# Seventeen projection blocks by seven half-size products, none beside the convolution; identity, rows and first weights load ahead of the other constants

## The reference

```python
for l in range(2):                       # first block
    h = rmsnorm(x, g[0])
    y = even_mixer(h, ...) if l % 2 == 0 else odd_mixer(h, ...)
    x = x + rmsnorm(y, g[1])
    x = x + rmsnorm(square(relu(rmsnorm(x, g[2]) @ w1)) @ w2, g[3])
# even: p = h @ w_in (5120 columns), gated linear attention and retention, y @ w_out
# odd:  p = h @ w_in (3080 columns), a convolution over positions, an mLSTM, y @ w_out
# second block
z = modulate(rms_norm(x, g), sh1, sc1) @ w_in      # 5120 columns: q k v, xb bg cg, gates
x = x + ga1 * ((gate_a * (attention(q, k, v) @ w_pa) + gate_b * (conv(xb, bg, cg) @ w_pb)) @ w_o)
x = x + ga2 * moe(modulate(rms_norm(x, g2), sh2, sc2))  # 32 experts, two for each row
```

## Time and profile before

| | |
|---|---|
| time, median of 3 runs | 1543.97 us (1541.52 to 1544.95) |
| time of the profiled execution | 1541.41 us |
| its span, first to last instruction | 1539.6 us |
| PE busy | 1301.7 us, 85% |
| DVE busy | 439.4 us, 29% |
| ACT busy | 194.2 us, 13% |
| POOL busy | 73.9 us, 5% |

### The profile page before, as it was taken

One profiled execution on the slowest core, in us unless ns is written; L12 is line 12 of the kernel. 1 busy time (PEld: TensorE's weight loads), 2 busy tenths in 40 slices (PEclk: granted clock), 3 DMA queues, 4 the chain that ended last, 5 costly groups with the idle time before them and its releaser, 6 DMA issues.

```text
span 1539.6 us, 12320 instructions
## 1 busy us (share of the span) xinstructions
PE 1301.7 (85%) x5308; PEld 706.0 (46%) x5308; DVE 439.4 (29%) x615; ACT 194.2 (13%) x274; POOL 73.9 (5%) x77
## 2 busy tenths in 40 slices
PE   7899998999999997999999999998746646646646
PEld 3455546886444453888444445445312212212212
DVE  3355122456442432246544130214101001001001
ACT  2321111111001321111001113101100000000000
POOL 0126101000000000000001100000000000000000
PEclk9999998999999999999999999999878868878788
DMA  9433332885453314587453443365699999999996
GB/s 333 145 110 123 151 110 101 309 299 192 164 178 105 133 76 158 182 299 264 168 187 136 171 156 110 123 259 231 283 429 427 428 427 427 427 428 427 427 428 258
DMA packets 93462, 376.72 MB, mean 245 GB/s; under 512 B 6976, under 2 KB 7520, under 8 KB 81504
## 3 DMA queue, kind: packets, MB, share of 16 engines
q1 hardware_dynamic: 92696, 373.80, 62.8%
q0 software_dynamic: 576, 2.10, 0.4%
q10 hardware_dynamic: 136, 0.04, 0.0%
HBM read 374.88 MB, written 1.05 MB: 244 GB/s over the span
## 4 chain that ended last, share of the span: by engine, by line
PE 74%; DMA 19%; DVE 2%; SPq 2%; issue 1%; ACT 1%; POOL 0%; POOLq 0%; DVEq 0%; ACTq 0%
PE PS L619 24%; PE PS L786 15%; PE PS L796 12%; DMA weights<-in_w 10%; DMA proj_rows<-in_w 9%; PE PS L644 8%; PE PS L1006 5%; PE PS L1037 2%; PE PS L589 1%; SPq L455 1%; PE PS L700 1%; PE PS L970 1%; PE PS L756 1%; PE PS L978 1%; PE PS L830 0%
## 5 line engine op out<-in xcount | busy, mean ns | idle before, releaser
L619 PE MATMUL PS<-weights,normalised 128*128 128x512 f32 x832 | 365.1, 598 | 2.4 <-DVE normalised L1354 2.2
L619 PEld LDWEIGHTS PS<-weights,normalised 128*128 128x128 f32 x832 | 158.1, 192 | 196.6 <-issue 196.6
L1006 PE MATMUL PS<-weights,arena 128*32 128x512 f32 x512 | 140.1, 708 | 114.2 <-DMA weights<-in_w 81.3
L786 PE MATMUL PS<-normalised,weights 128*128 128x256 f32 x1024 | 224.0, 382 | 1.7 <-DVE normalised L1354 1.7
L786 PEld LDWEIGHTS PS<-normalised,weights 128*128 128x128 f32 x1024 | 196.1, 192 | 29.4 <-DVE normalised L1354 2.3
L796 PE MATMUL PS<-weights,arena 128*128 128x512 f32 x384 | 167.4, 592 | 0.0
L644 PE MATMUL PS<-weights,arena 128*128 128x512 f32 x288 | 125.1, 593 | 5.4 <-issue 4.5
L1006 PEld LDWEIGHTS PS<-weights,arena 128*32 128x32 f32 x512 | 36.3, 128 | 185.5 <-issue 158.1
L796 PEld LDWEIGHTS PS<-weights,arena 128*128 128x128 f32 x384 | 73.0, 190 | 91.0 <-issue 90.9
L1006 PE MATMUL PS<-arena 128*32 128x512 f32 x208 | 72.3, 723 | 22.7 <-DMA proj_rows<-in_w 22.7
L1813 DVE TENSOR_TENSOR arena<-arena,PS 128x512 f32<-128x512 f32 x8 | 8.4, 1047 | 291.3 <-PE PS L1006 291.3
(11 more groups left out here) (282 smaller groups left out, 1088.5 us busy)
## 6 DMA issues: line engine op xcount, KB each, us to landing
weights<-in_w SPq DMA_DIRECT2D x41, 2048.0 KB, 25.7
weights<-in_mlp_w SPq DMA_DIRECT2D x32, 2048.0 KB, 7.9
arena<-in_w SPq DMA_DIRECT2D x21, 2048.0 KB, 24.9
proj_rows<-in_w SPq DMA_DIRECT2D x20, 2048.0 KB, 25.4
proj_rows<-in_w_ada SPq DMA_DIRECT2D x12, 2048.0 KB, 8.2
weights<-in_ev_w_in SPq DMA_DIRECT2D x10, 2048.0 KB, 8.3
weights<-in_w_in SPq DMA_DIRECT2D x10, 2048.0 KB, 7.9
normalised<-in_w SPq DMA_DIRECT2D x10, 2048.0 KB, 24.8
```

What stands on the lines that cost most here:

```text
L619: last = mm(PS[:, 2 * (n % 2) + tt, :], HT[:, k, tt * P:(tt + 1) * P], wn(s)[:, k, :], start=(k == 0), stop=(k == KT - 1))
L786: last = mm(PS[:, 4 + 2 * h + j // 2, (j % 2) * T:(j % 2 + 1) * T], wn(s)[:, k, j * P:(j + 1) * P], HT[:, k, :], start=(k == 0), stop=(k = ...
L1006: last = mm(PS[CAP * x:CAP * (x + 1), 4 + kind, :], XG[:, k, CAP * x:CAP * (x + 1)], w[:, k, :], start=(k == 0), stop=(k == KT - 1), tile_ ...
```

## The change

Seventeen of the 26 blocks (`SEVEN`: even blocks 1, 2, 3, 8, 9; odd blocks 1, 2, 3; blocks 1 to 9 of the second block) are multiplied by `seven_block`. Rows and columns are halved: four halves of the rows (128 rows x 512) and four of the block (512 x 256). DVE makes four sums of row halves once in each layer (`row_halves`) and four sums of weight halves for each block (`col_sums` three, `last_sum` one; one of them in place, the others in the fourth slot). PE makes seven products of four matmuls each, 128 x 128 against 128 x 256, 28 matmuls. Some products stay in PSUM and others are added onto them, so ACT reads four partial sums out while PE goes on (`part`), PE waits for those reads, DVE adds them (`part_sums`), and ACT does the rest (`finish`). The even blocks 4 to 7 and the odd blocks 4 and 5 stay as they were, and so does the first block of each layer.

The order of the even layer changes with it: block 3 now runs before the levels begin, the products of `hg_b` write banks 6 and 7, and the levels move one block on. At the start the identity is loaded alone and ahead of x, the first weights ahead of five of the rows, and the rest of the constants after the mask tables. Two gain rows (`ga_in`) are loaded in the first MLP. Expert block 0 is no longer loaded early; the slots of the first three expert blocks change places.

```diff
+SEVEN = ([B_EV_IN + b for b in (1, 2, 3, 8, 9)] + [B_OD_IN + b for b in range(1, 4)]
+         + B_IN2_AT[1:])
+SUM_BUFS = ((0, 2, 3), (3, 0, 2), (2, 3, 0))
-MOE_SLOTS = (3, 6, 7, 1, 4, 5, 2, 0, 8)
+MOE_SLOTS = (6, 7, 3, 1, 4, 5, 2, 0, 8)
...
+            sp.dma_start(IDN, A["keep"][:, 0:P]).then_inc(sem("const_in"), 16)
             for tt in range(TT):
                 sp.dma_start(X[:, tt, :], xv[:, tt, :]).then_inc(sem(f"x{tt}_in"), 16)
-            sp.dma_start(CK[:, :], A["keep"]).then_inc(sem("const_in"), 16)
-            row_loads(nc.sync, 0)
...
                 if b == 0:
+                    row_loads(nc.sync, ROW_LOADS[7:])
                     ld("lb_in", LB, A["hg_lower_bound"].partition_broadcast(P))
                 elif b == 1:
                     ld("mix_in", MX, A["mix"])
+                    ld("mix_in", CK[:, P:C_KEEP], A["keep"][:, P:C_KEEP])
...
-                if b == 3:
-                    sp.wait_ge(sem("block_used"), B_MLP1 + MLP_B)
-                    expert_load(0)
...
-            for j in range(1, 3):
-                sp.wait_ge(sem("block_used"), B_PB + 1)
-                expert_load(j)
+            sp.wait_ge(sem("block_used"), B_PB + 1)
+            expert_load(0)
+            expert_load(1)
             sp.wait_ge(sem("block_used"), B_IN2_AT[9] + 1)
+            expert_load(2)
             expert_load(3)
...
+            def seven_block(b):
...
+                pe.wait_ge(sem(f"slot{s}_full"), fulls(b))
+                pe.wait_ge(sem("row_sums"), 1 + (b >= B_OD_IN) + (b >= B_IN2))
+                pe.wait_ge(sem("col_sums"), 2 * m + 1)
+                pe.wait_ge(sem("proj_taken"), n - 1)
+                product(x, HT[:, 0:4, 0:P], b11, True).then_inc(sem("proj_part"), 1)
+                product(y, s1, t1, True).then_inc(sem("proj_part"), 1)
+                pe.wait_ge(sem("part_read"), 4 * m + 1)
+                product(x, s2, t2, False).then_inc(sem("proj_part"), 1)
+                pe.wait_ge(sem("part_read"), 4 * m + 2)
+                product(y, s4, b22, False)
+                pe.wait_ge(sem("part_read"), 4 * m + 3)
+                product(x, s3, t3, False).then_inc(sem("proj_part"), 1)
+                product(z, HT[:, 4:8, 0:P], b21, True).then_inc(sem("proj_part"), 1)
+                pe.wait_ge(sem("part_read"), 4 * m + 4)
+                pe.wait_ge(sem("col_sums"), 2 * m + 2)
+                product(x, HT[:, 4:8, P:T], t4, False).then_inc(sem("block_used"), 1)
...
-            for b, levels in ((3, (1,)), (4, (2, 3)), (5, (4, 5)), (6, (6, 7)), (7, (8,)), (8, ())):
+            for b, levels in ((4, (1, 2)), (5, (3, 4)), (6, (5, 6)), (7, (7, 8))):
                 proj_block(B_EV_IN + b)
...
+            def finish(b, cols, func=ACT.Copy, scale=1.0):
...
+                act.wait_ge(sem("part_sum"), m + 1)
+                act.wait_ge(sem("block_used"), b + 1)
+                last = a(PR[:, 1, cols:cols + T], PS[:, 2 * (n % 2), 0:T], func, scale=scale)
+                if func != ACT.Copy or scale != 1.0:
+                    top, low = PR[:, 0, cols:cols + NB], PR[:, 1, cols + T:cols + NB]
+                    a(top, top, func, scale=scale)
+                    last = a(low, low, func, scale=scale)
...
+            def col_sums(b):
...
+                dve.wait_ge(sem(f"slot{s}_full"), fulls(b))
+                if m:
+                    dve.wait_ge(sem("proj_part"), 5 * m - 4)
+                link(v.tensor_tensor(t3, b22, b12, ALU.subtract))
+                if m:
+                    dve.wait_ge(sem("proj_part"), 5 * m - 2)
+                link(v.tensor_tensor(t2, t3, b11, ALU.add))
+                tell(v.tensor_tensor(b12, b12, b11, ALU.subtract), "col_sums", 2 * m + 1)
...
+            def last_sum(b):
...
+                if m:
+                    dve.wait_ge(sem("proj_part"), 5 * m - 1)
+                v.tensor_tensor(t4, wn(slot_of(b))[:, 4:8, 0:T], t2, ALU.subtract).then_inc(sem("col_sums"), 1)
...
+            def part_sums(b, cols):
...
+                dve.wait_ge(sem("part_read"), 4 * m + 4)
+                dve.wait_ge(sem("proj_part"), 5 * m + 5)
```

More of the change, by code:

```diff
@@ L346, in block_program, with row_loads @@
         ]
-        def row_loads(queue, part):
-            for at, col, src in ROW_LOADS[part::2]:
+        def row_loads(queue, loads):
+            for at, col, src in loads:
                 queue.dma_start(AR[at:at + src.shape[0], col:col + P], src).then_inc(sem("rows_in"), 16)
@@ L889, in _ @@
                 logits(h)
[L890 removed]
+            seven_block(B_IN2_AT[5])
             pe.wait_ge(sem("at_s"), 8)
@@ L1095, in _ @@
             evac(0, ACT.Silu)
-            evac(NB, ACT.Sigmoid)
+            parts(B_EV_IN + 1)
+            finish(B_EV_IN + 1, NB, ACT.Sigmoid)
+            part(B_EV_IN + 2, 0)
+            part(B_EV_IN + 2, 1)
             act.wait_ge(sem("hg_qT_raw"), 1)
@@ L1123, in _ @@
             a(S01, PS[:, 4, :].rearrange("p (h t) -> p h t", h=4), ACT.Copy).then_inc(sem("hg_s01"), 1)
-            even_evac(8)
+            parts(B_EV_IN + 8)
+            finish(B_EV_IN + 8, 8 * NB, ACT.Silu)
             def squares(src, dst, wait, v, name):
@@ L1135, in _ @@
                   PS[:, 4 + half, :].rearrange("p (h t) -> p h t", h=4), ACT.Copy).then_inc(sem("ret_T"), 1)
-            even_evac(9)
+            parts(B_EV_IN + 9)
+            finish(B_EV_IN + 9, 9 * NB, ACT.Silu)
             n_mix = [0]
@@ L1200, in _ @@
             evac(0, ACT.Copy)
-            evac(NB, ACT.Copy)
+            parts(B_OD_IN + 1)
+            finish(B_OD_IN + 1, NB)
             act.wait_ge(sem("gates_raw"), 1)
@@ L1210, in _ @@
             a(GR[:, 2, :], GR[:, 1, :], ACT.Ln, bias=1.0).then_inc(sem("g_softplus"), 1)
-            evac(2 * NB, ACT.Copy)
+            parts(B_OD_IN + 2)
             for q in range(4):
@@ L1231, in _ @@
             mlp_square(1)
-            for b in range(2):
-                evac(b * NB, ACT.Copy)
+            IN = B_IN2_AT
+            evac(0, ACT.Copy)
+            parts(IN[1])
+            part(IN[2], 0)
+            part(IN[2], 1)
+            finish(IN[1], NB)
             a(HB.rearrange("p (a b) -> p a b", a=2), PR[:, :, 0:1024], ACT.Square).then_inc(sem("mix_sq"), 1)
-            for b in range(2, 4):
-                evac(b * NB, ACT.Copy)
+            part(IN[2], 2)
+            part(IN[2], 3)
+            parts(IN[3])
+            finish(IN[2], 2 * NB)
             for q in range(4):
@@ L1243, in _, with logit_exps @@
                   PS[:, 4 + q, :].rearrange("p (h t) -> p h t", h=4), ACT.Copy).then_inc(sem("qk_T"), 1)
-            evac(4 * NB, ACT.Copy)
-            act.wait_ge(sem("at_max"), 1)
-            for h in range(AH):
+            finish(IN[3], 3 * NB)
+            parts(IN[4])
+            def logit_exps(h):
                 a(AS[:, h, 0:P], AS[:, h, 0:P], ACT.Exp, bias=ST[:, 32 + h:33 + h], scale=AD ** -0.5,
@@ L1250, in _ @@
                   accum_out=ST[:, 56 + h:57 + h]).then_inc(sem("at_exp"), 1)
-            evac(5 * NB, ACT.Copy)
+            part(IN[5], 0)
+            part(IN[5], 1)
+            finish(IN[4], 4 * NB)
+            act.wait_ge(sem("at_max"), 1)
+            for h in range(2):
+                logit_exps(h)
+            part(IN[5], 2)
+            for h in range(2, 4):
+                logit_exps(h)
+            act.wait_ge(sem("at_max"), 2)
+            logit_exps(4)
+            part(IN[5], 3)
+            for h in range(5, AH):
+                logit_exps(h)
+            finish(IN[5], 5 * NB)
             for q in range(6):
@@ L1255, in _ @@
                     .then_inc(sem("at_pT"), 1)
-            evac(6 * NB, ACT.Sigmoid)
+            parts(IN[6])
             for tt in range(TT):
@@ L1260, in _ @@
                   ACT.Copy).then_inc(sem("u_T"), 1)
-            evac(7 * NB, ACT.Sigmoid)
+            part(IN[7], 0)
+            part(IN[7], 1)
+            finish(IN[6], 6 * NB, ACT.Sigmoid)
+            part(IN[7], 2)
+            part(IN[7], 3)
             for tt in range(TT):
@@ L1269, in _ @@
                     .then_inc(sem("u_T"), 1)
+            finish(IN[7], 7 * NB, ACT.Sigmoid)
             for b in range(8, 10):
-                evac(b * NB, ACT.Sigmoid)
+                parts(IN[b])
+                finish(IN[b], b * NB, ACT.Sigmoid)
             for half in range(2):
@@ L1644, in _ @@
             norm(GM[:, 0, :], MC[:, 0, :])
+            IN = B_IN2_AT
+            row_halves(IN[0])
+            for b in range(1, 3):
+                col_sums(IN[b])
+                last_sum(IN[b])
+            part_sums(IN[1], NB)
             dve.wait_ge(sem("mix_sq"), 4)
```

203 lines of the change are left out of this document (169 added, 34 removed).

## The result

Before 1542.74 us median of 4 runs, changed kernel 1526.58 (1525.64 to 1529.26): ratio 0.990, 95% interval 0.9883 to 0.9917. The change makes the kernel 16 us faster where 28.5 were forecast; 1526.58 lies 0.6 us above the range (1507 to 1526), and the gain is a little more than half of the forecast. The profiled execution took 1525.64 us with a span of 1523.8, against 1539.6: 15.8 us between the two profiles.

What follows compares the result with a forecast made beforehand. PE was taken to set the time until the expert-weight stream starts near 1093 us. 27.4 + 6.8 - 1.4 - 1.8 - 2.0 - 0.75 - 0.55 + 0.8 = 28.5 us saved, forecast 1514 us, range 1507 to 1526.

Steps and rivals of the forecast that it cites:

- The blocks: Seventeen seven-product blocks take 12.12 us each on PE instead of 13.73, saving 1.61 each, 27.4 us in all.
- Even layer, order: With block 3 ahead of the levels, PE's 9.99 us there become 3.6, plus 0.36 at the next block: 6.8 saved.
- The bound of 2 us for block 8's sums: Even block 8: DVE's sums beside POOL's rotations cost PE nothing, 2 us at the slowest.
- The Silu behind them: Finish of even block 8: its table load can no longer be made in advance, costing 0.15 us.
- Start: PE's start at 14.28 us was taken as unchanged, between 1 us sooner and 1 later.
- Odd layer: Its seven-product blocks save 4.8 us, less a 1.4 us wait in block 2: 3.4 us.
- the wait at the gates: Odd block 2: ACT works on the gates before its first read, so PE waits 1.4 us.
- Second block: Nine seven-product blocks, with waits of 1.8, 2.0 and 0.75 us and 0.8 won at block 7: 10.3 us gained.
- 5.87: Second block: the us POOL needs from the sums of squares of q and k to the norm.
- The stages without an edit: Both MLP stages and the stage from output product to experts hold no seven-product block; forecast change 0.
- The rival of half the gain: PE at half clock around waits near 893 and 897, several products waiting for reads: 18 us less gain, 1532; chance 0.12.
- the wait for q and k: Second block, `qk_ready` at 893.1 us, ahead of block 4: PE waits 1.8 us.

Runs made afterwards that it cites:

- e5: Changed kernel with all 26 projection blocks plain, keeping the new order, start and expert slots; 1536.0 us, ratio 0.9971 to the kernel before.
- e3: Changed kernel with the old start: all constants in one load, rows split over both queues ahead of the first weights; 1525.19 us, ratio 0.9886.
- e13: e11 with the five rows that SP loads put back ahead of the first weights; 1514.17 us, ratio 0.9814.
- e11: Changed kernel with even block 8 and block 3 of the second block plain (fifteen seven-product blocks); 1515.33 us, ratio 0.9830.
- e4: Changed kernel with block 3 of the second block plain (16 seven-product blocks); 1520.83 us, ratio 0.9858.
- e6: Changed kernel with matmuls on constants keeping PE busy at stage boundaries and the modulation's one-column products moved earlier; 1531.02 us, ratio 0.9930.
- e7: Kernel before the change with the same edit as e6; 1546.62 us, ratio 1.0033.
- e2: Kernel before the change run once more, nothing edited; one run, 1545.4 us.
- e8: Changed kernel with even block 8 plain; 1521.96 us, ratio 0.9869.
- e9: Changed kernel with two matmuls on constants (1.7 us) behind the odd layer's block 0; 1531.1 us, ratio 0.9926, its profile from an execution at 1524.39.
- e12: e11 with six matmuls on constants ahead of the transposes of both MLPs; 1516.6 us, ratio 0.9829.
- e1: Changed kernel run once more, nothing edited; 1527.4 us, ratio 0.9902 to the kernel before.
- e10: Changed kernel with four matmuls on constants (3.5 us) behind the odd layer's block 0; 1532.04 us, ratio 0.9929.
- e14: Changed kernel with all blocks of the second block plain, the eight seven-product blocks of the other two layers kept; 1535.09 us, ratio 0.9939.

## Why the prediction was wrong

**The blocks** (27.4 counted): right. Each takes 12.09 us, and seven products start one after another without a loss where the reads are on time. What the sum lacked stands around them, in two steps: the clock at the stage boundaries, and POOL's rate.

**Even layer, order** (6.8): right. 3.57 us instead of 9.99; e5 has it apart, 229.02 us from block 0 to the first MLP against 235.01, 6.0, though its blocks 0 and 1 take 30.66 us and not 29.40. (The prediction's upper end, 7.2 "if not even the 3.6 show", is a slip: its own rows give 9.99 + 0.36.) The bound of 2 us for block 8's sums was right and its value, 0, wrong: DVE turned to them 5.5 us ahead of the block and not 8, at 2.2 us each, and PE waits 1.31. The Silu behind them costs 6.33 - 5.92 = 0.4 and not 0.15.

**Start** (0, within 1): 1.24 in the profile. The rows behind 2 MB of weights land too late; x and its norms do not set that time. How much of it reaches the end stays small: the whole old start gives back 0.3 us at the first MLP (e3), the five rows alone 1.4 (e13), part of it by the clock in block 0 (13.97 us against 15.67 in e11).

**Odd layer** (3.4): 3.97, with 1.6 us for the wait at the gates (1.4 forecast). The half-clock stretch that made block 4 last 15.63 us before is gone, 1.7 us not foreseen; block 0 costs 0.7 more by the clock.

**Second block** (10.3): 5.4. Timeline of PE in the changed kernel around `qk_ready`:

```profile
884.76 3.28 PE L618 MATMUL PS<-constants,proj_rows 128*128 128x128 f32 x16 [3.29 <-DVEq L1887]
888.87 12.32 PE L665 MATMUL PS<-weights,normalised 128*128 128x256 f32 x56 [0.84 <-DVE weights L1540]
```

PE waits 3.3 us for q and k (1.8 forecast). Block 4 begins 60.3 us after block 0, where the forecast has 55.8. Of these 4.5 us block 0 makes 2.3, at half clock, and POOL 1.9: from the end of DVE's sums of squares to the norm pass 7.8 us and not 5.87. The 16 transposes take 3.28 us at half clock where they take 1.75, but that costs nothing, since PE waits another 0.84 behind them for block 4's sums; in e4 they take 1.91, and the wait grows to 1.48. The step that failed here is the rate of POOL: the 5.87 was taken from a stretch with DVE idle, and the change puts DVE's sums beside it (e4 takes them away, and POOL is back at 5.7 us, from 7.5).

**The stages without an edit** (0): 5.3 us. This is the step of the sum that failed by most: PE's clock at the stage boundaries, put at nothing without a row for it. With the 2.3 us in the second block and 0.8 and 0.7 at blocks 0 of the even and odd layer, some 9 us of the missing 12.7 stand in rows that do the same work as before in more time, at a granted clock near 0.5 (at even block 0, ahead of the clock's record, that is inferred from its 16.45 us against 15.67); 1.7 come back in odd block 4. The rest is POOL (1.9), block 8 (1.6) and the start (1.2), and about 0.6 are not placed. The prediction asked of the clock only whether the new waits would lower it. The rival of half the gain had this mechanism, but placed at 893 and 897 and inside the blocks; a stretch does stand behind the first of these, the wait for q and k, but costs nothing there.

That these stages follow the clock shows in the sixteen profiles. Two stages have the same work in each of them (e6 and e7, which add matmuls, are left out of the first):

| stage | half clock within it, us | its length, us | profiles |
|---|---|---|---|
| second MLP, to the second block | 5.8 to 6.7 | 219.84 to 220.22 | before, e2, e5, e8, e9, e11, e12, e13 |
| the same | 10.5 | 222.14 to 222.15 | changed, e1, e3, e4, e10, e14 |
| output product, to the experts | 6.8 | 56.95 to 57.12 | e5, e11 |
| the same | 10.2 or 13.7 | 58.59 to 58.69 | before, e2, e7, e8, e9, e12, e13 |
| the same | 20.5 | 61.23 to 61.40 | changed, e1, e3, e4, e6, e10, e14 |

The slots of the first expert blocks, which the change moved, don't decide the last stage: e5 and e11 have the changed ones and are the shortest. Within it the 32 records of one product (L1038, L970 before, L1039 in e5) take 6.41 us in the changed kernel, 5.47 before and 3.85 in e5.

What sets the length of these stretches stays open. Shown is that it isn't the seven-product blocks as such: all blocks of the second block plain (e14) keep the 61.4 us of the last stage, even block 8 plain (e8) brings 58.7. Shown too is that it can differ between two executions of one kernel (before and e2 have 3.4 and 6.8 us at the second MLP; e1 has a stretch at 565 that the first profile lacks), and that it is another in profiles of kernels edited far ahead (e8, e11); with one or two profiles for each kernel, which set is its usual one is read from the times alone. That the time of arrival at a boundary decides it is an argument from these, not a demonstration.

## What to carry to other kernels

A block with fewer products is worth having only where its sums find an idle engine. On the path, the one beside POOL's norm costs 2.9 us more than it saves, and the one beside POOL's rotations saves nothing. e13, without the two and with the rows loaded first, has almost twice the gain of the change (28.7 us by its ratio, against 16), but most of that extra is clock whose cause stays open (8.4 of the 11.6 us between e11 and e1). When a change shifts stages of a kernel on one core, its boundaries at half clock shift in length too, here by 8 to 9 us: widen the range by that, and compare an edit of a few us by the stage in the trace as well as by the median.

## What the runs showed of the hardware that was not expected

POOL is slowed by DVE as well as DVE by POOL: 32 elements on 128 partitions took 6.38 instead of 5.43 us, and the small instruction ahead 1.13 instead of 0.23, with DVE's sums at 1.22 beside them; beside POOL's rotations it was DVE's sums that took 2.2. The half-clock stretches at the stage boundaries had the same lengths in two profiles of the changed kernel, 10.2 us at the second MLP, but 6.8 with an edit 450 us earlier (e8); with it went 2.3 us in the MLP's product, 1.9 in the block behind and 2.6 in the last stage. Filling PE's wait with matmuls on constants took time off where it was done (the first MLP's product 113.00 to 110.77 us in e12), without a gain in the whole.
